# Last stage of a hybrid decoder layer: GpSimd's work moved to VectorE, and both requests' score products issued side by side

## The reference

```python
h = rmsnorm(x) ; p = h @ w_in
o = concat[NSA(p) * silu(z), GLA(p) * silu(z), ShortConv(p) * silu(z)]      # 512 | 256 | 256 columns
x = x + rmsnorm(o @ w_out)                                                  # for prompt and sample rows
# sample NSA: 8 heads x 64, 2 KV heads; compressed, selected and window branch
p_s = masked_softmax(einsum('bqhgd,bqhkd->bqhgk', q, k_selected)); o_s = p_s @ v_selected
# GLA: gated linear attention in chunks, S_t = diag(a_t) S_{t-1} + k_t^T v_t, o_t = q_t S_t
```

## Time and profile before

| | before |
|---|---|
| median of 3 runs | 1093.35 us (1092.61 to 1097.33) |
| profiled execution | 1089.71 us, span 1088.0 us |
| PE / DVE / ACT / POOL busy | 956.3 / 607.1 / 412.2 / 242.2 us |
| mean granted clock of TensorE | 0.949 |

### The profile page before, as it was taken

One profiled execution on the slowest core, in us unless ns is written; L12 is line 12 of the kernel. 1 busy time (PEld: TensorE's weight loads), 2 busy tenths in 40 slices (PEclk: granted clock), 3 DMA queues, 4 the chain that ended last, 5 costly groups with the idle time before them and its releaser, 6 DMA issues. The chain is left out here.

```text
span 1088.0 us, 16638 instructions
## 1 busy us (share of the span) xinstructions
PE 956.3 (88%) x5935; PEld 813.5 (75%) x5935; DVE 607.1 (56%) x1394; ACT 412.2 (38%) x892; POOL 242.2 (22%) x197
## 2 busy tenths in 40 slices
PE   3999999999799989998998799978288998989976
PEld 2999999999689877777898687764156565765654
DVE  3532010395435677886456787864954666576640
ACT  4532111111224455665244465653432343333311
POOL 3019599998100000000002300000700000000001
PEclk9899999999899999999899899998688999999988
DMA  6226534433331110000110142014224453452310
GB/s 198 86 79 207 186 133 143 153 116 98 110 94 56 34 34 8 1 1 8 41 47 22 36 117 79 1 38 149 77 71 121 136 146 113 119 160 66 92 37 29
DMA packets 106676, 93.73 MB, mean 86 GB/s; under 512 B 21101, under 2 KB 99810, under 8 KB 104482
## 3 DMA queue, kind: packets, MB, share of 16 engines
q1 hardware_dynamic: 84946, 58.65, 18.0%
q10 hardware_dynamic: 19344, 17.25, 5.4%
q0 software_dynamic: 2304, 16.78, 4.4%
HBM read 78.16 MB, written 18.61 MB: 89 GB/s over the span
## 5 line engine op out<-in xcount | busy, mean ns | idle before, releaser
L588 PE MATMUL ps<-w_hi,h_hi 128*128 128x264 f32 (+5 forms) x432 | 125.1, 289 | 1.1 <-DVE h_lo L457 1.1
L588 PE MATMUL ps<-w_lo,h_hi 128*128 128x264 f32 (+5 forms) x432 | 124.0, 287 | 0.0
L588 PE MATMUL ps<-w_hi,h_lo 128*128 128x264 f32 (+5 forms) x432 | 123.9, 287 | 0.0
L1276 DVE TENSOR_TENSOR pt_lo<-ps,pt_hi 128x512 fp32r<-128x512 f32 x132 | 90.8, 688 | 50.7 <-ACT pt_hi L1192 49.9
L1192 ACT ACTIVATE pt_hi<-ps 128x512 fp32r<-128x512 f32 x132 | 78.5, 597 | 79.2 <-PE ps L1099 78.4
L465 DVE TENSOR_TENSOR w_lo<-w_raw,w_hi 128x1024 fp32r<-128x1024 f32 (+2 forms) x12 | 32.1, 2679 | 120.9 <-ACT w_hi L366 120.9
L1272 DVE TENSOR_REDUCE least<-ps 128x1 f32<-128x640 f32 (+7 forms) x128 | 89.9, 702 | 12.1 <-PE ps L1088 10.7
L313 POOL TENSOR_TENSOR chunk<-chunk 128x1024 f32<-128x1024 f32 (+2 forms) x46 | 81.9, 1780 | 3.6
L588 PEld LDWEIGHTS ps<-w_hi,h_hi 128*128 128x128 f32 (+1 forms) x432 | 80.7, 187 | 1.8 <-ACT h_hi L357 1.0
L1958 POOL TENSOR_TENSOR y_row<-y_row,x_row 128x1024 f32<-128x1024 f32 (+1 forms) x8 | 19.2, 2406 | 277.4 <-DVE y_row L2606 277.4
L588 PEld LDWEIGHTS ps<-w_lo,h_hi 128*128 128x128 f32 (+1 forms) x432 | 80.8, 187 | 0.0
(11 more groups left out here) (374 smaller groups left out, 2404.6 us busy)
## 6 DMA issues: line engine op xcount, KB each, us to landing
kv_pages<-in_cache_slc_kv SPq DMA_DIRECT2D x256, 64.0 KB, 1.9
shared<-in_x_prompt SPq DMA_DIRECT2D x8, 512.0 KB, 3.6
w_raw<-in_w_in SPq DMA_DIRECT2D x8, 512.0 KB
wr_raw<-in_w_in SPq DMA_DIRECT2D x8, 512.0 KB, 4.0
kv_window<-in_cache_win_kv SPq DMA_DIRECT2D x4, 1024.0 KB, 5.6
wo_raw<-in_w_out SPq DMA_DIRECT2D x8, 512.0 KB, 8.2
out<-in_cache_win_kv SPq DMA_DIRECT2D x1, 4032.0 KB
x_row<-in_x_prompt ACTq DMA_DIRECT2D x7, 512.0 KB, 4.7
```

The source lines that it names most:

```text
L588: mm = nc.tensor.matmul(out, lhs, rhs, start=(k == 0 and i == 0), stop=(k == KD - 1 and i == 2))
L1276: nc.vector.tensor_tensor(pt_lo[:, t % PTS, :], ps[:, turn_bank(t), :], pt_hi[:, t % PTS, :].bitcast(F32), ALU.subtract).then_inc(s_ptl, 1)
```

## The change

Five things, all in `tail`. The GpSimd block is gone: VectorE computes `wo_lo`, and the residual. Both requests' score products of a chunk are one step, issued next to each other, and `turned` has three buffers in place of two. The end of an output tile is cut into halves of 512 columns: ScalarE squares a half when its eight `out` steps are done, VectorE multiplies it with the weight `post`, ScalarE takes one root, and one VectorE instruction scales and adds x. The last two tiles' `out` steps form one list instead of two, and only the gating of the last tile stays a list of its own. The table of costs has other numbers (for `values`, `o`, `update`, `scores` and others), which changes the order everywhere in the stage. Some small tiles also move to another place in SBUF.

```diff
@@ def pair(pi) @@
-        yield "turn_k", pi, 0
-        for n in range(2 * NCK):
-            if n + 1 < 2 * NCK:
-                yield "turn_k", pi, n + 1
-            yield "scores", pi, n
+        for n in range(3):
+            yield "turn_k", pi, n
+        for c in range(NCK):
+            yield "scores", pi, c
+            for n in range(2 * c + 3, min(2 * c + 5, 2 * NCK)):
+                yield "turn_k", pi, n
@@ project_out @@
             for g in range(GROUPS):
                 yield "out", m, g
+                if g % KD == KD - 1:
+                    yield "half", m, g // KD
...
+            yield "root", m, 0
             yield "resid", m, 0
@@ def parts(step) @@
-            "scores": (("PE", 0.52), ("DVE", 0.7)) if y % 2 else (("PE", 0.52),),
+            "scores": (("PE", 0.95), ("DVE", 0.7)),
-            "values": (("PE", 0.65),) if y < NCK else (("PE", 0.1), ("DVE", 1.4)),
+            "values": (("PE", 1.05),) if y < NCK else (("PE", 0.43), ("DVE", 1.4)),
-            "o": (("PE", 0.7), ("DVE", 0.42)),
+            "o": (("PE", 4.6 if x == S else 1.35), ("DVE", 0.42)),
@@ block.gpsimd: taken out @@
-            @block.gpsimd
-            def _(pool):
-                for what, x, y in order["POOL"]:
...
-                        nc.gpsimd.tensor_tensor(wo_lo[:, x, :], wo_raw[:, x, :], wo_hi[:, x, :].bitcast(F32),
-                                                ALU.subtract).then_inc(s_wl, 1)
...
-                        nc.gpsimd.tensor_tensor(yt[q][0:R, :], yt[q][0:R, :], xr[q][0:R, :], ALU.add
-                                                ).then_inc(s_y[q], 1)
@@ block.tensor @@
                     elif what == "scores":
-                        b, c = y % 2, y // 2
-                        if b == 0:
-                            scored(SPP * x + 1 + c)
-                        mm = nc.tensor.matmul(ps[half(b), SC, :], q_pair(x)[:, half(b)], turned_of(("k", x, y)),
-                                              start=True, stop=True)
-                        if b == 1:
-                            mm.then_inc(s_sc, 1)
+                        scored(SPP * x + 1 + y)
+                        kT0, kT1 = [turned_of(("k", x, 2 * y + b)) for b in range(2)]
+                        nc.tensor.matmul(ps[half(0), SC, :], q_pair(x)[:, half(0)], kT0, start=True, stop=True)
+                        nc.tensor.matmul(ps[half(1), SC, :], q_pair(x)[:, half(1)], kT1, start=True, stop=True
+                                         ).then_inc(s_sc, 1)
@@ block.scalar @@
+                    elif what == "half":
+                        act.wait_ge(s_op, 2 * x + y + 1)
...
+                        nc.scalar.activation(yt[q][0:R, 512 * y:512 * y + 512], ps[0:R, out_bank[q] + y, :], ACT.Square,
+                                             scale=D ** -0.5, accum_out=rr[:, y:y + 1]).then_inc(s_sq2, 1)
+                    elif what == "root":
+                        act.wait_ge(s_of, 2 * x + 1)
+                        act.wait_ge(s_sq2, 2 * x + 2)
+                        did(nc.scalar.activation(rr[:, 2:3], rr[:, 1:2], ACT.Ln, bias=rr[:, 0:1]))
+                        nc.scalar.activation(rr[:, 2:3], rr[:, 2:3], ACT.Exp, scale=-0.5).then_inc(s_rr, 1)
@@ block.vector @@
+                    if what == "w_split":
+                        dve.wait_ge(s_wh, x + 1)
+                        nc.vector.tensor_tensor(wo_lo[:, x, :], wo_raw[:, x, :], wo_hi[:, x, :].bitcast(F32),
+                                                ALU.subtract).then_inc(s_wl, 1)
...
+                    elif what == "half":
+                        cols = slice(512 * y, 512 * y + 512)
+                        dve.wait_ge(s_sq2, 2 * x + y + 1)
...
+                        nc.vector.tensor_tensor(yt[q][0:R, cols], ps[0:R, out_bank[q] + y, :], post[0:R, cols],
+                                                ALU.mult).then_inc(s_of, 1)
+                    elif what == "resid":
+                        dve.wait_ge(s_of, 2 * x + 2)
+                        dve.wait_ge(s_rr, x + 1)
+                        dve.wait_ge(s_x[q], 16 * m + 16)
+                        nc.vector.scalar_tensor_tensor(yt[q][0:R, :], yt[q][0:R, :], rr[:, 2:3], xr[q][0:R, :],
+                                                       ALU.mult, ALU.add).then_inc(s_y, 1)
```

More of the change, by code:

```diff
@@ L1570, in parts @@
             "o_back": (("SP", 3.0),),
-            "turn_mix": (("PE", 1.3), ("DVE", 1.2), ("ACT", 1.05)),
+            "turn_mix": (("PE", 0.66), ("DVE", 1.2), ("ACT", 1.05)),
             "mix_lo": (("DVE", 1.2),),
-            "out": (("PE", 0.72),) if y < GROUPS - 1 else (("PE", 0.72), ("ACT", 1.9), ("DVE", 1.3)),
+            "out": (("PE", 0.72),),
+            "half": (("ACT", 0.6), ("DVE", 0.7 if y else 0.85)),
+            "root": (("ACT", 0.55),),
             "load_x": (("ACT", 0.2),),
-            "resid": (("POOL", 2.4),),
+            "resid": (("DVE", 1.2),),
             "store_y": (("ACT", 0.1),),
-            "w_load": (("SP", 20.0),),
-            "w_split": (("ACT", 1.05), ("POOL", 2.5)),
+            "w_load": (("SP", 18.0),),
+            "w_split": (("ACT", 1.05), ("DVE", 1.15)),
         }
@@ L1705, in needs @@
                 else:
-                    on(*(("out", x - 1, GROUPS - 1) if x else ("update", S, DB - 1)), "DVE")
+                    on(*(("half", x - 1, 1) if x else ("update", S, DB - 1)), "DVE")
                 if x == OWN:
@@ L1717, in needs @@
             if x == 0:
-                on("w_split", y % KD, 0, "POOL")
-        elif what == "out" and eng == "ACT" and 0 < x < LASTM:
-            on("store_y", x - 1, 0, "ACT", 4.0)
+                on("w_split", y % KD, 0, "DVE")
+        elif what == "half" and eng == "ACT":
+            on("out", x, KD * (y + 1) - 1, "PE")
+            if y == 0 and 0 < x < LASTM:
+                on("store_y", x - 1, 0, "ACT", 4.0)
+        elif what == "root":
+            on("half", x, 0, "DVE")
         elif what == "w_split":
@@ L1724, in needs @@
             if x > 0:
-                on("resid", x - 1, 0, "POOL")
+                on("resid", x - 1, 0, "DVE")
             else:
@@ L1728, in needs @@
         elif what == "store_y":
-            on("resid", x, 0, "POOL")
+            on("resid", x, 0, "DVE")
         elif what == "resid":
-            on("out", x, GROUPS - 1, "DVE")
+            on("root", x, 0, "ACT")
             on("load_x", x, 0, "ACT", 5.0)
@@ L1736, in schedule @@
         HANDOVER = 0.15
-        lists = [list(decays()), list(linear()), list(sample_states()), [s for pi in range(PAIRS) for s in pair(pi)], list(project_out(range(LASTM))),
-                 list(project_out([LASTM])), list(split_out())]
+        lists = [list(decays()), list(linear()), list(sample_states()), [s for pi in range(PAIRS) for s in pair(pi)], list(project_out()),
+                 list(gated(LASTM)), list(split_out())]
         heads, after, before = {}, {}, {}
@@ L1769, in path @@
             return left[key]
-        order = {eng: [] for eng in ("PE", "ACT", "DVE", "POOL", "SP")}
+        order = {eng: [] for eng in ("PE", "ACT", "DVE", "SP")}
         free, at = dict.fromkeys(order, 0.0), {}
@@ L2177, in _ @@
                         if k == KD - 1:
[L2178 removed]
+                            mm.then_inc(s_op, 1)
             @block.scalar
@@ L2190, in copy @@
                     act.wait_ge(s_tb, m + 1)
-                    nc.scalar.activation(turned[0:rows, m % 2, 0:n], ps[0:rows, TN, 0:n], ACT.Copy).then_inc(s_tbe, 1)
+                    nc.scalar.activation(turned[0:rows, m % 3, 0:n], ps[0:rows, TN, 0:n], ACT.Copy).then_inc(s_tbe, 1)
                 def load_v(n):
@@ L2308, in _ @@
                         nc.scalar.activation(sg[0:R, 4:8], sg[0:R, 4:8], ACT.Exp, scale=-0.5).then_inc(s_r4, 1)
-                    if what in ("turn_mix", "out"):
+                    if what in ("turn_mix", "half", "root"):
                         R = rows_out[x]
                         q, m = turn_of(x)
-                        rr = sg[0:R, 8 + 3 * q:11 + 3 * q]
+                        rr = sg[0:R, 8 + 3 * (x % 2):11 + 3 * (x % 2)]
                     if what == "turn_mix":
                         act.wait_ge(s_mf[q], m + 1 + GATED * q)
-                        ge(act, s_op[q], 2 * m)
+                        if q == 0:
+                            ge(act, s_op, 2 * x)
@@ L2425, in _ @@
                                                 ).then_inc(s_sct, 1)
-                    elif what == "scores" and y % 2 == 1:
-                        c = y // 2
+                    elif what == "scores":
+                        c = y
                         dve.wait_ge(s_sc, (NCK + 3) * pi + 2 + c)
@@ L2442, in _ @@
                         combine(pi, 0)
-                    elif what == "w_scores" and y == 1:
+                    elif what == "w_scores":
                         dve.wait_ge(s_sc, (NCK + 3) * pi + 2 + NCK)
@@ L2586, in _ @@
                                                 ).then_inc(s_mix, 1)
```

(7 more changed lines are left out.)

129 lines of the change are left out of this document (60 added, 69 removed).

## The result

The changed kernel takes 1069.05 us (median of 4 runs, 1065.59 to 1070.45) against 1094.0 before (1092.61 to 1097.33). The ratio is 0.9752, with a 95% interval of 0.972 to 0.9784. That is a gain of 25 us where 45 were forecast, outside the range on the slow side.

A forecast was written before the change was run, and what follows sets the result against it. TensorE was taken as the bound, through work, gaps and clock. Terms 14 + 12 + 5 + 3 + 4 + 3 + 4.2 = 45 us gave 1044.5 us profiled, 1048 by the median; forecast 1038 to 1056, range 1032 to 1064.

The forecast's parts named there:

- Without the 18.7 us gap the clock should not fall twice between 762 and 826: Behind the opening: of 8.3 us lost there to TensorE's low clock 3 stay, a gain of 5 us, bounds 0 and 8.
- GpSimd's work on VectorE: Opening: VectorE no longer stands still beside GpSimd, so TensorE's 15.7 us wait shrinks; gain 14 us, bounds 6 and 15.7.
- Score products: Both requests' products run at the same time: 17 us less TensorE work, less waits for copies; gain 12 us.
- Rival A: ScalarE's copies between transposes bind: scores save 8 in place of 12, softmax comes later; 1054 to 1060 us, chance 0.15.
- The gap at 808: From 808 to 826, short GLA steps wait on one another; pair work around them gains 3 us, between 0 and 6.
- output tiles: Boundaries between tiles: banks emptied earlier by halves, and vanished stalls; gain 4 us, between -8 and 10.
- the gap at 1044: Before the last tiles: tile 7's gating first, the last tile's hidden; gain 3 us, mainly clock, bounds 0 and 8.
- Rival B: VectorE's in-order list binds, residuals delaying the next gating: no gain or a loss; chance 0.03 up to a 5 us gain.
- The end: After TensorE's last product: the tail falls from 10.2 to 6.0 us, a gain of 4.2 us.

The follow-up runs named there:

- The fillers: Changed kernel with useless identity transposes added to TensorE's list ahead of its waits: 1055.26 us with 29 gaps filled, 1053.87 with only the 14 long ones.
- split alone: Kernel before with only the eight `wo_lo` of the opening made by VectorE in place of GpSimd: 1084.29 us, ratio 0.9868 to the kernel before.
- all but the scores: Changed kernel with the score products put back as before, one request's at a time, and their old prices: 1081.43 us, ratio 0.9872 to the kernel before.
- scores alone: Kernel before with both requests' score products next to each other, three turned buffers and their two prices: 1082.55 us, ratio 0.988 to the kernel before.
- six such lists: Changed kernel and five variants with another hand-over time, later residual, both, or old planner prices, the same instructions in other orders: 1060.55 to 1074.0 us.

## Why the prediction was wrong

By kinds of loss, the sum said: work -17, idle time -16 (14 and 3 in the opening, 4 at the tiles, less 5 for the waits on copies), clock -8 (5 behind the opening, 3 at 1044), end -4.2. The traces say: -18.9, -9.4, +10.9, -4.3. Of the 26 us between 45.2 and 19.3, the clock is 19. By the medians, 20 us are missing (25 for 45), and the clock with the later start is about 16 of them, by the estimate of 7.6 us more where 8 less were forecast. Either way it is the largest part.

**The step that failed: "Without the 18.7 us gap the clock should not fall twice between 762 and 826".** It took the one large gap as the cause of the clock's falls. The trace has it at 0.62 over 786 to 808, a stretch with waits of 1.69 and 2.80 us. It fell shortly behind the first one and stayed at the lower level, 0.50, from 792 to 800 although TensorE was busy for all of these 8 us (first and last row: waits; the others: stretches, as in the tables of the stage). It was at that level for some us at a time all through the middle too, behind waits of mostly 1.9 to 3.9 us and once, at 876, behind one of 0.82.

```profile
789.97 0.33 PE L1967 MATMUL ps<-ident,prob_s 128*128 128x128 f32 x1 [1.69 <-ACT turned L2189]
...
790.00:792.00 2.00, 2.00 (x20) 1.48 (x20) 0.83 (x5) 0.36 (x2) 0.00 (x0) 0.83 0.51 144
792.00:800.00 8.00, 8.00 (x26) 5.81 (x25) 3.30 (x12) 0.96 (x3) 0.00 (x0) 0.50 0.63 200
...
804.27 1.22 PE L2003 MATMUL ps<-cs_s,same 128*128 128x256 f32 x2 [2.80 <-DVE cs_s L2409]
```

The bounds, 0 and 8, left a loss out altogether, though the rows showed the clock falling behind the much smaller gap at 1044 too. The fillers show that the gaps of about 1 us and more are the main cause: with them filled, 20 of 31 us come back, and the four executions have a granted clock of 0.960 to 0.972 where the changed kernel's have 0.940 to 0.945. The scores taken alone also paid clearly more to the clock than the kernel before, 35.0 us against 20.4; for "split alone" (22.4) and "all but the scores" (28.9) the excess is within what executions differ by, or nearly so. The order alone moves this loss as well, from 18.6 to 34.1.

**GpSimd's work on VectorE: 14.** The premise was right in its pieces: prices, the vanished stall, VectorE's total (201 against 203). But the bound of 15.7 us was too high: with the stall gone the wait could lose only 9.6, as shown at "split alone", and the rest had to come from work that moved into it. Up to the first `out` the idle time fell by 14.1 us, in "split alone" by 10 of its 30.6. But the first `out` product came at 817, not 803: the stage began 2.4 us later, the clock cost 2.5 more where 5 less were expected, and idle time fell by 14 where 17 were expected.

**Score products: 12.** Right in number, and measured alone: 12 to 13. Work is 19 less for 17, and the waits of TensorE for `turned` rose from 7.0 us (5.4, 1.1 and 0.5 in the waits of before) to 13.6, by 6.6 for my 5. But that the net came out is partly luck: in "scores alone" these waits rose by 6.3 us while idle time as a whole fell by 1.7, and what took the rest of the 19.6 us of work was the clock, to which this term gave nothing. Rival A, whose mark was 15 us, did not come about. By the Trainium skill, "TensorEngine Tiling (Array Packing)", PSUM Bottleneck, the copy may become the bottleneck; the trace has the waits, but the 2.67 us one is due to DMA issues ahead of the copy, and filling the short ones changed nothing (1068.88).

**The gap at 808, output tiles, the gap at 1044: 3 + 4 + 3.** The gap behind 1044 is gone, but behind the first `out` idle time rose by 4.7 us in all: from 970 to 1034 stand waits of 3.90 and 3.17 us for `m_lo`, 1.55 for the banks' second half and 3.13 for `qB`, all late in VectorE's list. "Scores alone", whose output tiles are those of before, has the same rise (22.2 to 27.9). So it isn't the tiles' own edits alone. I read it as lost cover: TensorE has 19 us less to do while the same chains run on VectorE and ScalarE. That is argued, not shown. Rival B, VectorE's list as the bound, was right in kind at these places and far too dear.

**The end: 4.2.** Right, 4.3.

**The order.** The range didn't allow for it. Where the planner's list changes, what TensorE has to do at each wait changes too, and six such lists spread over 13 us. The forecast's 1038 to 1056 was narrower than fits that, even with every term right.

## What to carry to other kernels

Keep an account of the bottleneck engine in three columns, work, idle and clock, by slices, before and after: work taken off an engine that waits in places comes back in part as idle time and as clock, and only a forecast with the last two in it, with both signs, holds. Where waits of 1 us and more can't be removed, cheap useless products in them can be worth more than the useful work that one saves: 12 to 15 us here, for a few lines and a table of 14 places. When a planner sets the order, run two or three lists with the same work before judging an edit worth less than their spread. And look at the granted clock of every execution before two traces are compared: the one profiled can be the lucky one.

## What was not expected of the hardware

- 117 added transposes, 19 us by their price in the changed kernel and 14.7 in the account, made the kernel 15 us faster when they stood in long idle times; 108 added products outside the idle times cost 23 us.
- Filling the idle times of less than 1 us left the median where it was (1068.88 against 1069.05), while the clock's loss in the trace went from 31.3 to 27.5 us and the work up by 3.8.
- The last stage began between 729.0 and 737.5 us in the profiled executions, though nothing ahead of it differs. Over 0 to 728 the granted clock is 0.98 in the first of these and 0.96 in the second; the account gives 12.2 and 21.3 us of clock ahead of the stage, with the work the same within 1 us.
